# Two small loads are issued at the start of the kernel, and six small transposes of modulation rows move one projection unit forward

## The reference

```python
silu_c = silu(c); silu_cc = silu(c_ctx)
for l in range(2):
    sh1, sc1, g1, sh2, sc2, g2 = split(silu_c @ ada_w[l] + ada_b[l], 6)        # likewise for the context
    h = rms_norm(x, norm1_g[l]) * (1 + sc1) + sh1
    # layer 0: project h to q, k, v of 8 neighbourhood heads and 4 differential heads (1024 x 3072 weights)
    qa, ka, va, qb, kb, vb = split(h @ w_in, 6)     # q and k: rms_norm per head with gains na_q_g, ..., rope on qb, kb
    x = x + g1 * (attention(...) @ w_out)
    x = x + g2 * channel_mix(rms_norm(x, norm2_g[l]) * (1 + sc2) + sh2)   # swiglu; layer 1: top-2 of 8 experts
```

## Time and profile before

| | |
|---|---|
| time, median of 3 runs | 1963.69 us (1963.4 to 1964.03) |
| time of the profiled execution | 1963.69 us |
| its span, first to last instruction | 1961.9 us |
| PE busy | 1835.4 us, 94% of the span |
| DVE, ACT busy | 1376.3 us (70%), 1109.6 us (57%) |
| mean granted TensorE clock | 0.977 of full speed |
| start, up to the first product of the projection | 0 to 49.3 us |
| projection of layer 0 | 49.3 to 215 us |

### The profile page before, as it was taken

The page is one execution under the profiler, slowest core; times in us unless marked ns, Lnnn a source line. Parts: engine busy times, 40 slices in busy tenths (PEclk is TensorE's granted clock), DMA queues, the critical chain, the costliest instruction groups (busy, mean ns, idle before and its releaser), DMA issues.

```text
span 1961.9 us, 24617 instructions
## 1 busy us (share of the span) xinstructions
PE 1835.4 (94%) x8626; PEld 1434.3 (73%) x8626; DVE 1376.3 (70%) x1769; ACT 1109.6 (57%) x1479; POOL 168.3 (9%) x247
## 2 busy tenths in 40 slices
PE   5999878799999997969889999999999999999999
PEld 2777554388888886636778888888888888888877
DVE  2533665576645456273579898898989999899887
ACT  3423474132222323256368887878778888888684
POOL 0114121001100100433000000000000000000110
PEclk8999999899999998999889999999999999999999
DMA  9244500468464542310279999999999999999995
GB/s 357 97 171 172 161 1 1 150 245 311 140 199 136 199 163 83 107 65 1 86 274 379 367 387 373 375 386 376 384 367 375 390 375 395 366 385 376 386 353 208
DMA packets 231537, 496.38 MB, mean 253 GB/s; under 512 B 6064, under 2 KB 43952, under 8 KB 231472
## 3 DMA queue, kind: packets, MB, share of 16 engines
q1 hardware_dynamic: 227936, 488.53, 68.2%
q0 software_dynamic: 1920, 5.77, 0.9%
q10 hardware_dynamic: 1616, 1.22, 0.2%
HBM read 475.05 MB, written 20.45 MB: 253 GB/s over the span
## 4 chain that ended last, share of the span: by engine, by line
PE 73%; DVE 10%; DMA 7%; ACT 5%; issue 4%; SPq 1%; POOL 0%; DVEq 0%; ACTq 0%; POOLq 0%
PE ps L2017 7%; PE ps L2019 7%; PE ps L2018 7%; PE ps L1880 6%; PE ps L1882 6%; PE ps L1881 6%; DMA ring<-in_moe_w 6%; PE ps L2031 4%; PE ps L2030 4%; PE ps L2029 4%; PE ps L1847 4%; DVE wlo L1547 3%; PE ps L1776 2%; PE ps L1736 2%; PE ps L1738 2%
## 5 line engine op out<-in xcount | busy, mean ns | idle before, releaser
L1547 DVE TENSOR_TENSOR wlo<-ring,whi 128x1024 fp32r<-128x1024 f32 x672 | 796.4, 1225 | 92.2 <-ACT whi L1120 81.8
L1120 ACT ACTIVATE whi<-ring 128x1024 fp32r<-128x1024 f32 x672 | 691.5, 1057 | 202.1 <-DMA ring<-in_moe_w 80.2
L2017 PE MATMUL ps<-whi,xgr 128*128 128x512 f32 x896 | 354.4, 396 | 1.5 <-DVE xgr L1610 1.5
L2019 PE MATMUL ps<-whi,xgr 128*128 128x512 f32 x896 | 350.3, 391 | 0.0
L2018 PE MATMUL ps<-wlo,xgr 128*128 128x512 f32 x896 | 349.9, 391 | 0.0
L2019 PEld LDWEIGHTS ps<-whi,xgr 128*128 128x128 f32 x896 | 168.7, 188 | 35.8
L2017 PEld LDWEIGHTS ps<-whi,xgr 128*128 128x128 f32 x896 | 168.9, 188 | 35.4 <-issue 1.7
L2018 PEld LDWEIGHTS ps<-wlo,xgr 128*128 128x128 f32 x896 | 169.0, 189 | 34.1
L1084 ACT ACTIVATE fsa<-ring 128x1024 fp32r<-128x1024 f32 (+2 forms) x76 | 71.8, 946 | 192.7 <-PE ps L1882 192.6
L2029 PE MATMUL ps<-whi,hidr 128*128 128x512 f32 x448 | 175.9, 393 | 0.0
L2031 PE MATMUL ps<-whi,hidr 128*128 128x512 f32 x448 | 174.7, 390 | 0.0
(11 more groups left out here) (249 smaller groups left out, 2590.3 us busy)
## 6 DMA issues: line engine op xcount, KB each, us to landing
ring<-in_moe_w SPq DMA_DIRECT2D x168, 2048.0 KB, 9.7
ring<-in_ada_w SPq DMA_DIRECT2D x24, 2048.0 KB, 12.6
ring<-in_ev_w_in SPq DMA_DIRECT2D x6, 2048.0 KB, 8.0
ring<-in_ffn_w_gate SPq DMA_DIRECT2D x11, 1024.0 KB, 5.4
ring<-in_ffn_w_up SPq DMA_DIRECT2D x11, 1024.0 KB, 8.0
expert_tokens<-work SPq DMA_DIRECT2D x2, 3072.0 KB, 18.2
ring<-in_ffn_w_down SPq DMA_DIRECT2D x4, 1536.0 KB, 8.7
ring<-in_ffn_w_down SPq DMA_DIRECT2D x4, 1280.0 KB, 8.4
```

Of the source, the lines that this page charges most:

```text
L1120: act.activation(whi[:, u % URING, :], mslot[(u // 4) % MRING][:, (u % 4) * UNIT:(u % 4 + 1) * UNIT], ACT.Copy).then_inc(m_hi, 1)
L1547: dve.tensor_tensor(wlo[:, u % URING, :], mslot[(u // 4) % MRING][:, (u % 4) * UNIT:(u % 4 + 1) * UNIT], whi[:, u % URING, :].bitcast(F32) ...
L2017: pe.matmul(bank[:, :], xgr[:, 0, kk, :], hi[:, ws], start=(kk == 0), stop=False)
L2019: ins = pe.matmul(bank[:, :], xgr[:, 1, kk, :], hi[:, ws], start=False, stop=(kk == KT - 1))
```

## The change

There are three edits. (1) The loads of `vec` and `rtr` are issued by ScalarE right behind the other three, and count on `s_cst`, which now goes to 80; `s_vec` is gone. VectorE's first wait and TensorE's wait between the first two modulation chunks are for 80 now. (2) VectorE scales the gains and makes the dot products at its start, ahead of the reciprocal of the first norm. (3) In the projection loop `ada_turn` stands one step earlier, after unit 4c+3 where it stood after unit 4c+4, and `ada_take` after unit 4c+4 where it stood after 4c+5. ScalarE's order in the loop is not touched.

```diff
--- before.py
+++ after.py
@@ -344,7 +344,6 @@
         s_x = sem("x_loaded")
         s_cond = sem("conditioning_loaded")
         s_cst = sem("constants_loaded")
-        s_vec = sem("gains_and_router_loaded")
         eps_set = sem("eps_set")
         s_bt = sem("bias_loaded")
         s_ones = sem("ones_set")
@@ -909,6 +908,8 @@
             act.dma_start(adab[:, :, :].rearrange("p a b -> p (a b)"), a["adab"]).then_inc(s_cst, 16)
             act.dma_start(ng[:, :, :, :].rearrange("p a b c -> p (a b c)"), a["ng"]).then_inc(s_cst, 16)
             act.dma_start(cst[:, :], a["cst"]).then_inc(s_cst, 16)
+            act.dma_start(vec[:, :], a["vec"].partition_broadcast(P)).then_inc(s_cst, 16)
+            act.dma_start(rtr[:, :, :], a["moe_router"].rearrange("(k p) n -> p k n", p=P)).then_inc(s_cst, 16)
             act.wait_ge(s_cond, 16)
             act.wait_ge(s_czero, 1)
             act.activation(scond[:, :, 0:2], v3(cond[:, :], 2), ACT.Silu).then_inc(s_scond, 1)
@@ -1029,8 +1030,6 @@
                 act.activation(sq[k % 4], xT[:, k, :], ACT.Square).then_inc(norm["n00"]["square"], 1)
             act.wait_ge(eps_set, 1)
             root("n00", S_ALL, KT)
-            act.dma_start(vec[:, :], a["vec"].partition_broadcast(P)).then_inc(s_vec, 16)
-            act.dma_start(rtr[:, :, :], a["moe_router"].rearrange("(k p) n -> p k n", p=P)).then_inc(s_vec, 16)
             for j in range(4):
                 act.wait_ge(ada_used, j + 1)
                 if j >= 2:
@@ -1179,7 +1178,16 @@
         def _(dve):
             ch = Chain(dve, d_step)
             dve.memset(eps[:, :], EPS).then_inc(eps_set, 1)
-            dve.wait_ge(s_cst, 48)
+            dve.wait_ge(s_cst, 80)
+
+            for n in ("na_q_g", "diff_q_g", "gqa_q_g"):
+                dve.tensor_scalar(vv(n), vv(n), HD ** -0.5, None, ALU.mult)
+            dve.tensor_scalar(vv("mla_q_g"), vv("mla_q_g"), float(MLA_QK) ** -0.5, None, ALU.mult)
+            dve.tensor_scalar(vv("diff_subln_g"), vv("diff_subln_g"), 1.0 - LAM_INIT, None, ALU.mult).then_inc(gain_rd, 1)
+            dots = tn[2]
+            ch.after(dve.tensor_tensor(dots[:, 0:64], vv("diff_lq1"), vv("diff_lk1"), ALU.mult))
+            ch.after(dve.tensor_tensor(dots[:, 64:128], vv("diff_lq2"), vv("diff_lk2"), ALU.mult))
+            dve.tensor_reduce(lamt[:, 0:2], v3(dots[:, 0:128], 64), AX.X, ALU.add).then_inc(lam_in, 1)
 
             def lam_dve():
 
@@ -1399,15 +1407,6 @@
                         ch.after(ins)
 
             norm_recip("n00", S_ALL)
-            dve.wait_ge(s_vec, 32)
-            for n in ("na_q_g", "diff_q_g", "gqa_q_g"):
-                dve.tensor_scalar(vv(n), vv(n), HD ** -0.5, None, ALU.mult)
-            dve.tensor_scalar(vv("mla_q_g"), vv("mla_q_g"), float(MLA_QK) ** -0.5, None, ALU.mult)
-            dve.tensor_scalar(vv("diff_subln_g"), vv("diff_subln_g"), 1.0 - LAM_INIT, None, ALU.mult).then_inc(gain_rd, 1)
-            dots = tn[2]
-            ch.after(dve.tensor_tensor(dots[:, 0:64], vv("diff_lq1"), vv("diff_lk1"), ALU.mult))
-            ch.after(dve.tensor_tensor(dots[:, 64:128], vv("diff_lq2"), vv("diff_lk2"), ALU.mult))
-            dve.tensor_reduce(lamt[:, 0:2], v3(dots[:, 0:128], 64), AX.X, ALU.add).then_inc(lam_in, 1)
             dve.wait_ge(ada_tr, 4)
             dve.tensor_tensor(adam[:, 0:16, :], ps[7][:, 0:32].rearrange("p (m c) -> p m c", c=2),
                               adabm[:, 0:16].unsqueeze(2).to_broadcast([P, 16, 2]), ALU.add).then_inc(ada_rd, 1)
@@ -1440,7 +1439,7 @@
 
             def between(x):
                 c = x // 4
-                if x % 4 == 1 and c >= 1:
+                if x % 4 == 0 and c >= 1:
                     ada_take(c - 1)
                 if x % 4 >= 2 and c < 5:
                     for i in (2 * (x % 4) - 4, 2 * (x % 4) - 3):
@@ -1716,7 +1715,7 @@
                         pe.wait_ge(ada_row, j - 1)
                     ada_chunk(at["A0a", j], ps[j % 2])
                     if j == 0:
-                        pe.wait_ge(s_cst, 48)
+                        pe.wait_ge(s_cst, 80)
                     else:
                         ada_turn(j - 1, adar[(j - 1) % 2], 8 * (j - 1))
                 ada_turn(3, adar[1], 24)
@@ -1861,10 +1860,10 @@
                 c = x // 4
                 if x % 4 == 2 and c < 6:
                     ada_chunk(at["A0b", c], ps[6])
-                if x % 4 == 0 and c >= 1:
-                    if c >= 2:
-                        pe.wait_ge(take_rd, c - 1)
-                    ada_turn(RING + c - 1, adar0, 0)
+                if x % 4 == 3 and c < 6:
+                    if c >= 1:
+                        pe.wait_ge(take_rd, c)
+                    ada_turn(RING + c, adar0, 0)
 
             proj_pe("L0", between)
             pe.wait_ge(take_rd, 6)
```

## The result

| | before | changed |
|---|---|---|
| median | 1963.74 us (7 runs) | 1974.27 us (7 runs, 1971.68 to 1981.91) |
| ratio, 95% interval | | 1.0059 [1.0044, 1.0076] |
| profiled execution | 1963.69 us | 1975.38 us |
| its span | 1961.9 us | 1973.6 us |
| mean granted clock in it | 0.977 | 0.970 |

The account below looks back on a forecast made before the run. TensorE was taken as the bound, 73% of the chain. To 1963.69 us came 4 x 0.6 = 2.5 for the longer waits, 0 for start and for chunks 2 and 5: 1966.2 us, range 1963.2 to 1969.6.

Parts of the forecast that it names:

- Start, 0: Start of the kernel: the earlier loads delay the tokens by at most 2.1 us, TensorE's 2.65 us of waiting absorbs it; 0.
- rival B: Start: clock stays up until the fourth chunk, whose 3.53 us halve; 2.5 us won in all, 1963.7; chance 13%.
- Chunks 2 and 5, 0: Projection, chunks holding v: rows are ready at the turn's new place too; 0, between -0.1 and +0.1 us.
- The wait at four places, 0.6 each: Projection, after units 3, 7, 15, 19: hole of 1.86 us traded for 2.57; 0.6 us each, 2.5 in all.
- The clock, taken as 1.00: Projection: clock reads 1.00 from 52 to past 215 us, so the sum holds no cost for falls.
- rival A: Projection's new holes: the clock falls, 1.6 us per fall; 1967.8 with one, 1972.6 with four; chance 35%.
- the two stretches of attention: 3.4 us with 0.30 busy, followed by 3.4 us at clock 0.50; 2.6 us with 0.35 busy, which kept 1.00.
- "full work on both sides": Sign against a clock fall: a hole in the projection has full work before and after it; no size given.
- "all four": Within rival A: the clock falls at all four places in the projection, 1972.6 us; no separate chance given.
- "one": Within rival A: the clock falls at one place in the projection, 1967.8 us; half of its 35%.
- The forecast: Whole kernel: 1966.2 us, up 0.13%, own range 1964.8 to 1967.4; chance 47%.

## Why the prediction was wrong

- *Start, 0.* Right in its parts: the fourth chunk landed at 35.00, the tokens came 1.97 us later (at most 2.1 forecast), the slack swallowed it, `rtr` was there at 15.5 (15 forecast). In the profiled execution the start was 1.7 us quicker by rival B's mechanism (chunk product at the upper clock), of which 1.3 were lost again when the projection began with 5.8 us at the lower clock instead of 2.9. That isn't bound to the change: with early loads the projection began anywhere from 47.66 to 51.22 in the other profiled executions, and the loads alone measure 0.9995.
- *Chunks 2 and 5, 0.* Right: 1.0008, not to be told from 1.
- *The wait at four places, 0.6 each.* Right: the turn waits 2.3 to 2.4 us four times, the mid-unit waits are gone, and with the clock held up by extra products 2.3 us are left of it in the stage, against 2.5.
- *The clock, taken as 1.00.* This step failed. The sum was made for four new holes without a fall, and a fall stood beside it as rival A, with 35% and half of that for one fall alone. All four fell, in all three profiled executions with the earlier turn and an unfilled hole. The size was short too: I priced a fall at 1.6 us, for 3.4 us at half speed, and four at 6.4; two of the four lasted 6.8, and the four together cost 9.5. At the first place the turn's own products ran at half speed as well, at the third a part of them. At the first place unit 3 ended 0.3 us earlier than before, so unit 5 was due at 84.5 and came at 87.5, 3.0 us late: 0.9 us from the turn (1.74 to the next product, 0.82 in the earlier trace rows) and 2.1 from the eleven products behind it, at 0.43 instead of 0.23.
- *Which row should have decided.* I held the two stretches of attention in the earlier trace rows against each other (the prediction calls them and the products at the lower clock; the two numbers are exchanged there), and let "full work on both sides" speak against a fall. The row of 3.4 us with 0.30 busy was the near one: the new hole is 2.3 us idle and 0.8 us of products of two columns, 3.1 us in which the array does next to nothing. The other one, at 836, isn't of attention but of a later projection (L1776, waiting for GpSimd). And I had read a shorter stretch in attention that fell, and left it out:

```profile
275.00:277.30 2.30, 0.37 (x4) 0.01 (x2) 1.77 (x4) 2.30 (x7) 1.03 (x2) 1.00 0.00 0
277.52:280.93 3.41, 3.41 (x24) 2.74 (x20) 0.40 (x3) 1.65 (x5) 2.69 (x4) 0.50 0.00 0
```

TensorE waits 1.93 us there, and 0.2 us behind the wait the clock is down, though the engine is busy then. The work ahead of it was less dense than in the projection (19.15 of the 24.8 us before it busy), so it doesn't settle the case, but it shows that a fall did not need 3 us. The four new holes are alike, so their falls are not four independent chances; I should have given the case "all four" its weight (it stood at 1972.6, within 2 us of the result), and not the case "one".
- *The chances.* The forecast, B and a tenth of A add up to 0.635 and not to the 0.61 that stands there; nothing hangs on it.

The Trainium skill (TensorE: Matmul & The Clock Gate, "HAM oscillation") says that bursts separated by waits start at the low clock each time; its example has waits of 3 to 5 us. I cited it and set it aside because the kernel before kept 1.00 through four holes of 1.7 us. The traces agree with it for holes shorter than its example: 2.3 us idle and the turn, twelve times of twelve.

## What to carry to other kernels

Before an instruction is moved forward, look when its input is ready and which work behind it was the cover of another wait; move the producer first (here ScalarE's copy), then the consumer. On TensorE count light products with the idleness next to them, and price a hole near 3 us in dense work with a fall of the clock, beside its own length; all twelve such holes fell, so weigh "all of them" as a case. Shorter ones, from 2.2 us on, may fall or not. Products that nobody needs, put into the hole for one run, tell the clock from the wait.

## What the runs showed of the hardware

- A hole of 2.3 us idle and 0.8 us of two-column products between dense stretches dropped the clock to 1.2 GHz twelve times out of twelve in three profiled executions; holes of 1.7 us idle in mid-unit (in the kernel before, with the loads alone, and with the earlier turn for chunks 2 and 5 alone) did so none of twelve times, and holes of 0.9 us idle behind the turn's 0.8 none of four. For 1.35 us idle with the turn it was four of four in one execution, for 2.3 us idle alone two of four.
- In the first of these twelve the clock fell after 2.0 us of idleness, before any two-column product; in attention it fell at the end of a wait of 1.93 us.
- The drop lasted 3.4 or 6.8 us, though TensorE was fully busy from the hole's end on. The four of 6.8 us are those that began earliest, ahead of the turn or within its first 0.5 us.
- Ten products of 512 columns more in each of four places cost nothing that can be measured (ratio to the kernel before 1.0000), and saved about 9 us against leaving TensorE idle (1965.0 us against 1973.87 with the earlier turn alone, on the same chip).
